# The second head's turn moved ahead of the first head's values, and the last stage moved inside the experts' programs

## The reference, cut to what matters

```python
y = mixer(u)                 # mLSTM heads and 4 latent-attention heads, one output projection
x = post_ln(alpha * x + (1 + g1) * y)            # alpha = 2 ** 0.25
u = layernorm(x) * (1 + sc2) + sh2
y = hier_moe(u)              # top-1 group of 4, then top-2 of its 8 experts
x = post_ln(alpha * x + (1 + g2) * y)            # the output

# latent attention, for a block of 128 queries and one head
s = qn @ kn.T + qr @ kr.T
p = softmax(s * scale)
o = p @ v

# gated experts: every token has two (expert, weight) pairs
out[e] = (silu(x @ w_gate[e]) * (x @ w_up[e])) @ w_down[e]
y[token] = w0 * out[e0][token] + w1 * out[e1][token]
```

## Time and profile before

| | us |
|---|---|
| time, median of 3 runs | 1618.43 (1618.35 to 1618.6) |
| time of the profiled execution | 1616.71 |
| its span | 1614.8 |
| PE busy | 1464.7 (91%) |
| DVE busy | 570.7 (35%) |
| ACT busy | 355.0 (22%) |
| attention loop, first turn to last values | 547 to 747 |
| last block's light down product ends | 1547.6 |
| first transfer of the last stage is issued | 1559.6 |

### The profile page before, as it was taken

One profiled execution on the slowest core, in us unless ns is written; L12 is line 12 of the kernel. 1 busy time (PEld: TensorE's weight loads), 2 busy tenths in 40 slices (PEclk: granted clock), 3 DMA queues, 4 the chain that ended last, 5 costly groups with the idle time before them and its releaser, 6 DMA issues. The chain is left out here.

```text
span 1614.8 us, 19679 instructions
## 1 busy us (share of the span) xinstructions
PE 1464.7 (91%) x7275; PEld 811.3 (50%) x7276; DVE 570.7 (35%) x1134; ACT 355.0 (22%) x735; POOL 97.1 (6%) x96
## 2 busy tenths in 40 slices
PE   5999999979969899998999269999999999999968
PEld 2555554448858456655555244444444444444423
DVE  1122127557749434334776621111111111011117
ACT  2122122146524333433111001011111110110111
POOL 0000011000000000000000011111111111011100
PEclk8999999999979999999999569999999999999979
DMA  9201011228710200003111089969789879999936
GB/s 377 99 27 39 0 7 41 54 75 246 241 56 1 105 0 0 0 0 141 53 66 66 26 343 374 408 236 370 314 345 392 312 317 410 423 358 419 401 149 275
DMA packets 98181, 305.49 MB, mean 189 GB/s; under 512 B 18065, under 2 KB 53053, under 8 KB 88920
## 3 DMA queue, kind: packets, MB, share of 16 engines
q1 hardware_dynamic: 89880, 287.08, 46.0%
q0 software_dynamic: 8064, 16.80, 2.8%
q10 hardware_dynamic: 192, 1.03, 0.2%
HBM read 289.86 MB, written 25.76 MB: 195 GB/s over the span
## 5 line engine op out<-in xcount | busy, mean ns | idle before, releaser
L385 PE MATMUL ps<-w_in_tok,uT 128*128 128x512 f32 (+2 forms) x512 | 191.5, 535 | 1.9 <-ACT uT L317 1.9
L1709 PE MATMUL ps<-w_gate_sb,x_slotsT 128*128 x320 | 144.4, 605 | 9.6 <-issue 9.6
L1725 PE MATMUL ps<-w_down_sb,hidT 128*128 x320 | 148.0, 605 | 0.0
L385 PEld LDWEIGHTS ps<-w_in_tok,uT 128*128 128x128 f32 x512 | 97.7, 192 | 90.2 <-issue 59.6
L1709 PE MATMUL ps<-w_up_sb,x_slotsT 128*128 x320 | 140.6, 592 | 0.0
L1913 DVE TENSOR_TENSOR hid<-silu_g,ps 128x512 f32<-128x512 f32 x20 | 13.8, 688 | 295.4 <-PE ps L1709 295.4
L1420 PE MATMUL ps<-uT,hT 128*128 128x512 f32 x256 | 114.1, 599 | 0.0
L529 PE MATMUL ps<-uT,mod 128*128 128x512 f32 x256 | 111.0, 593 | 0.8 <-PEq L204 0.8
L1709 PEld LDWEIGHTS ps<-w_gate_sb,x_slotsT 128*128 128x128 f32 x320 | 59.9, 192 | 86.9 <-issue 86.9
L1709 PEld LDWEIGHTS ps<-w_up_sb,x_slotsT 128*128 128x128 f32 x320 | 60.8, 190 | 76.5 <-issue 76.5
L1725 PEld LDWEIGHTS ps<-w_down_sb,hidT 128*128 128x128 f32 x320 | 57.5, 189 | 66.5 <-issue 65.6
(11 more groups left out here) (376 smaller groups left out, 1829.6 us busy)
## 6 DMA issues: line engine op xcount, KB each, us to landing
light_gate_sb<-in_w_gate SPq DMA_DIRECT2D x20, 2048.0 KB
light_up_sb<-in_w_up SPq DMA_DIRECT2D x20, 2048.0 KB
light_down_sb<-in_w_down SPq DMA_DIRECT2D x20, 2048.0 KB, 12.9
w_gate_sb<-in_w_gate SPq DMA_DIRECT2D x12, 2048.0 KB, 11.4
w_up_sb<-in_w_up SPq DMA_DIRECT2D x12, 2048.0 KB, 15.6
w_down_sb<-in_w_down SPq DMA_DIRECT2D x12, 2048.0 KB
mod<-in_w_ada SPq DMA_DIRECT2D x8, 1024.0 KB, 8.7
w_ada_late<-in_w_ada SPq DMA_DIRECT2D x8, 1024.0 KB, 7.8
```

The costliest lines, as they stand in the source:

```text
L385: mm = nc.tensor.matmul(ps[:, 2 + g, 0:n], self.uT[:, k, t * P:(t + 1) * P], wt[:, k, c0:c0 + n], start=k == 0, stop=k == KD - 1)
L1709: m = m_.matmul(ps[:, bank, :], xT[:, k, :], wt[:, bass.ds(buf, 1), k, :].rearrange("p a f -> p (a f)"), start=k == 0, stop=k == KD - 1)
L1725: m = m_.matmul(ps[:, 5 + half, :], hT[:, k, :], wd[:, bass.ds(buf, 1), k, half * 512:half * 512 + 512].rearrange("p a f -> p (a f)"), sta ...
```

## The change

In `attend`, PE turns the second head before it computes the values of the first, and DVE copies the second head's half before it scales the first head's output. The waits for the copies move out of `out`. ACT's program stays as it is.

The last stage loses its block. Its code follows the loop in every engine's program of `experts`, its tiles of x go into the gate weights' buffer, its expert rows into the buffers of `wu`, `lwg` and `lwu`, and its results into that of `wd`, each with room for all 8 tiles. The tiles of x are loaded after the last gate product (`s_G`), the expert rows after the last scatter has landed. PE has four pairs of banks for the sums instead of two, and does the residual part (alpha times x) up to three tiles ahead of the expert rows. The two rows of parameters `ln2_g` and `ln2_b` are loaded at the start of the block instead of after SP's loop.

```diff
                 def out(n, h):
                     j = h % 2
-                    pe.wait_ge(s_td, n + 1)
-                    pe.wait_ge(s_ta, n + 1)
                     pe.wait_ge(s_oe, n + 1)
...
                         scores(1 - g)
+                        pe.wait_ge(s_td, n + 1)
+                        pe.wait_ge(s_ta, n + 1)
+                        turn(1)
                         out(n, 2 * g)
-                        turn(1)
+                        pe.wait_ge(s_td, n + 2)
+                        pe.wait_ge(s_ta, n + 2)
                         out(n + 1, 2 * g + 1)
...
                         maximum(0)
                         maximum(1)
+                        turned(n + 1, 1)
                         out(n, t, 2 * g)
-                        turned(n + 1, 1)
                         out(n + 1, t, 2 * g + 1)
...
             @block.sync
+                sp.dma_start(self.g2[:], self.i["ln2_g"].partition_broadcast(P)).then_inc(self.s_again, 16)
+                sp.dma_start(self.b2[:], self.i["ln2_b"].partition_broadcast(P)).then_inc(self.s_again, 16)
...
...
+                sp.wait_ge(s_G, n + 1)
+                for t in range(TT):
+                    sp.dma_start(x1[:, t], self.x1d[t * P:(t + 1) * P, :]).then_inc(s_x1[t], 16)
+                sp.wait_ge(s_yfree, n + 1)
+                sp.wait_ge(s_lyfree, n + 1)
+                for t in range(TT):
+                    sp.dma_start(yt(t), yb[t]).then_inc(s_y[t], 16)
+                for t in range(TT):
+                    sp.wait_ge(s_o, t + 1)
+                    sp.dma_start(self.out[t * P:(t + 1) * P, :], z[:, t]).then_inc(s_st, 16)
...
             @block.tensor
+                def residual(t):
+                    if t > 3:
+                        pe.wait_ge(s_read, t - 3)
+                    pe.wait_ge(s_x1[t], 16)
+                    for half in range(2):
+                        m_.matmul(sums(t, half), al[:], x1[:, t, half * 512:half * 512 + 512], start=True, stop=False)
+                def rows_of_experts(t):
+                    pe.wait_ge(s_y[t], 16)
+                    pe.wait_ge(s_dg, 2 * t + 2)
+                    for k in range(2):
+                        for half in range(2):
+                            m = m_.matmul(sums(t, half), dg[:, t % 2, k, :], yt(t)[:, k, half * 512:half * 512 + 512], start=False, stop=k == 1)
+                    m.then_inc(s_sum, 1)
...
+                residual(0)
+                pe.wait_ge(s_sg, n + 1)
+                pe.wait_ge(s_h, n + 1)
+                residual(1)
+                pe.wait_ge(s_lh, n + 1)
+                pe.wait_ge(s_yd, n + 1)
+                residual(2)
+                pe.wait_ge(s_lyd, n + 1)
+                for t in range(TT):
+                    rows_of_experts(t)
+                    if t + 3 < TT:
+                        residual(t + 3)
```

More of the change, by code:

```diff
@@ L177, in build @@
             self.experts()
-            self.combine()
     def c(self, at, n=P, parts=P):
@@ L1531, in experts @@
         HF = FE // 2
+        s_x1 = [self.sem(f"x1_loaded{t}") for t in range(TT)]
+        s_y = [self.sem(f"pair_loaded{t}") for t in range(TT)]
+        s_cv, s_var, s_std, s_o, s_st = (self.sem(n) for n in ("cb_dve", "varC", "stdC", "out_ready", "out_stored"))
+        s_al, s_dg, s_sum, s_read = self.sem("alpha_diagonal"), self.sem("weight_diagonals"), self.sem("rows_summed"), self.sem("sum_read")
+        yb = self.ybuf.rearrange("(t p k) d -> t p k d", p=P, k=2)
+        SUM_BANKS = (0, 2, 6, 4)
         with ExitStack() as x, nc.Block() as block:
@@ L1573, in experts @@
             col = sb("table_cols", [P, 5])
+            al, dg = sb("alpha_diag", [P, P]), sb("weight_diag", [P, 2, 2, P])
+            st, mv, ve = sb("stC", [P, 2, 6]), sb("mvC", [P, 2]), sb("veC", [P, 2, 2])
+            x1 = wg[:].rearrange("p a k f -> p (a k f)").rearrange("p (t d) -> p t d", t=TT)
+            z = wd[:].rearrange("p a k d -> p (a k) d")
+            pairs = [buf.rearrange("p (t k d) -> p t k d", k=2, d=D) for buf in (
+                wu[:].rearrange("p a k f -> p (a k f)"), lwg[:].rearrange("p k f -> p (k f)"), lwu[:].rearrange("p k f -> p (k f)"))]
+            yt = lambda t: pairs[0][:, t] if t < 4 else pairs[t // 2 - 1][:, t % 2]
+            sums = lambda t, half: ps[:, SUM_BANKS[t % 4] + half, :]
             s_used = (s_G, s_U, s_Y)
@@ L1603, in _ @@
                                          src[bass.ds(e, 1)].rearrange("a p k f -> p (a k) f")).then_inc(s_w[j], 16)
-                sp.dma_start(self.g2[:], self.i["ln2_g"].partition_broadcast(P)).then_inc(self.s_again, 16)
-                sp.dma_start(self.b2[:], self.i["ln2_b"].partition_broadcast(P)).then_inc(self.s_again, 16)
+                sp.wait_ge(s_G, n + 1)
[8 more added lines that the diff above has]
+                    sp.dma_start(self.out[t * P:(t + 1) * P, :], z[:, t]).then_inc(s_st, 16)
+                sp.wait_ge(s_st, 16 * TT)
             @block.gpsimd
@@ L1761, in _ @@
                     m.then_inc(s_lY, 1)
+                def residual(t):
[11 more added lines that the diff above has]
+                    m.then_inc(s_sum, 1)
+                pe.wait_ge(s_al, 1)
+                pe.wait_ge(s_xT, n + 1)
+                pe.wait_ge(s_lxT, n + 1)
+                residual(0)
[10 more added lines that the diff above has]
+                        residual(t + 3)
             @block.scalar
@@ L1765, in _ @@
                 a = nc.scalar
+                ident = self.c(C_ID)
+                a.mul(al[:], ident, ALPHA).then_inc(s_al, 1)
                 act.wait_ge(s_d, 1)
@@ L1787, in _, with diagonals @@
                     a.copy(xlT[:].rearrange("p k t -> p (k t)"), ps[:, 0, 0:KD * LC]).then_inc(s_lxT, 1)
+                def diagonals(t):
+                    if t > 1:
+                        act.wait_ge(s_sum, t - 1)
+                    for k in range(2):
+                        a.mul(dg[:, t % 2, k, :], ident, self.wts[:, k, t:t + 1]).then_inc(s_dg, 1)
+                diagonals(0)
+                for t in range(TT):
+                    if t + 1 < TT:
+                        diagonals(t + 1)
+                    act.wait_ge(s_var, t + 1)
+                    a.activation(ve[:, t % 2, 1:2], ve[:, t % 2, 0:1], ACT.Sqrt).then_inc(s_std, 1)
             @block.vector
@@ L1926, in _ @@
                     v.tensor_tensor(yl[:], ps[:, 4, 256:256 + Q], gate2q[:], ALU.mult).then_inc(s_lyd, 1)
[L1927 to L2007, removed]
@@ L2008, in _ @@
+                cb = Chain(dve, s_cv)
                 dve.wait_ge(self.s_again, 32)
                 for t in range(TT):
-                    b, j = t % B, t % 2
-                    rows = ps[:, 2 * j:2 * j + 2, :].rearrange("p a b -> p (a b)")
+                    j, bank = t % 2, SUM_BANKS[t % 4]
+                    rows = ps[:, bank:bank + 2, :].rearrange("p a b -> p (a b)")
                     dve.wait_ge(s_sum, t + 1)
-                    ch.link(v.bn_stats(st[:, 0, :], ps[:, 2 * j, :]))
@@ L2014, in _ @@
-                    ch.link(v.bn_stats(st[:, 1, :], ps[:, 2 * j + 1, :]))
-                    ch.link(v.bn_aggr(mv[:], st[:].rearrange("p a b -> p (a b)")))
+                    cb.link(v.bn_stats(st[:, 0, :], sums(t, 0)))
+                    cb.link(v.bn_stats(st[:, 1, :], sums(t, 1)))
+                    cb.link(v.bn_aggr(mv[:], st[:].rearrange("p a b -> p (a b)")))
                     v.tensor_scalar_add(ve[:, j, 0:1], mv[:, 1:2], LN_EPS).then_inc(s_var, 1)
-                    if t >= B:
-                        dve.wait_ge(s_st[b], 16 * (t // B))
@@ L2019, in _ @@
-                    v.scalar_tensor_tensor(out=z[:, b], in0=rows, scalar=mv[:, 0:1], in1=g2[:], op0=ALU.subtract, op1=ALU.mult).then_inc(s_read, 1)
+                    v.scalar_tensor_tensor(out=z[:, t], in0=rows, scalar=mv[:, 0:1], in1=self.g2[:], op0=ALU.subtract, op1=ALU.mult).then_inc(s_read, 1)
                     dve.wait_ge(s_read, t + 1)
                     dve.wait_ge(s_std, t + 1)
-                    ch.link(v.reciprocal(ve[:, j, 1:2], ve[:, j, 1:2]))
-                    v.scalar_tensor_tensor(out=z[:, b], in0=z[:, b], scalar=ve[:, j, 1:2], in1=b2[:], op0=ALU.mult, op1=ALU.add).then_inc(s_o, 1)
+                    cb.link(v.reciprocal(ve[:, j, 1:2], ve[:, j, 1:2]))
@@ L2027 @@
+                    v.scalar_tensor_tensor(out=z[:, t], in0=z[:, t], scalar=ve[:, j, 1:2], in1=self.b2[:], op0=ALU.mult, op1=ALU.add).then_inc(s_o, 1)
 SHAPES = {
```

## The result

The changed kernel takes 1598.49 us (median of 4 runs, 1595.71 to 1601.71) against 1618.51 before, a ratio of 0.9876 with an interval of 0.9855 to 0.9896, so 20.0 us less. The profiled execution took 1597.24 us, its span is 1595.4 (before: 1616.71 and 1614.8).

| stretch, us | before | after |
|---|---|---|
| start to the first turn of attention | 546.97 | 545.70 |
| attention, first turn to the end of the last values | 199.74 | 189.79 |
| from there to the first matmul of the router's ranking | 167.59 | 168.21 |
| from there to the end of the last light down product | 633.31 | 633.10 |
| from there to the end of the span | 67.19 | 58.60 |

What follows compares the result with a forecast made beforehand. PE, busy nine tenths of the span, was taken as the bound, with its waits in attention and before the last stage. Attention 9.5 plus last stage 11.0 gave 20.5 us, so 1597.9 us; forecast 1595 to 1602, range 1594 to 1606.

Steps and rivals of the forecast that it cites:

- the loop step: Attention, step over the loop's end: its excess of 0.74 us goes, 7 steps, 5.2 us; 3.4 if only the wait goes.
- DVE's order: Attention: the second head's copy starts right behind both maxima, gaining 0.27 us for each of 16 groups, 4.3 us.
- (b): Last stage: residuals of three tiles, 5.2 us, fit before the rows land; PE leaves its loops in 3 to 4 us.
- (c): Last stage, low clock after PE's gap: about 1 us in the sum, with 0 and 2.7 as bounds.
- (a): Last stage, expert rows: first load issued at about 1552.0, takes 4.6 to 5.6 us, rows there at 1556.6 to 1557.6.
- (d): Last stage, final tiles: DVE sets the end, 39.5 us from the first sum on instead of 40.7, gaining 1.2 us.
- PE arrives late: Rival, last stage: PE leaves its loops only at 1559.6; time 1607.3, half as late 1602 to 1603; chance 0.15.
- the 1.5 us for seven rounds: Last stage: by the skill's branch times, seven empty loop rounds cost PE about 1.5 us, not 3 to 4.
- The loop step keeps its excess: Rival, attention: the 0.74 us is loop control, not ACT; 5.2 us less gain, 1603.1 us; chance 0.12.
- PE becomes the bound of attention: Rival, attention: needs the copy ahead of the maxima; 10.1 us more gain, 1587.8 us; chance 0.03.
- Reads of PSUM collide: Rival, attention: ACT's probabilities and DVE's maximum slow each other; 1628.3 us with maximum and copy doubled; chance 0.03.

Runs made afterwards that it cites:

- Experiment 1: Only the attention edits (PE's and DVE's order) made in the kernel before, last stage as it was: 1606.47 us against 1617.36, ratio 0.9941.
- experiment 3: Changed kernel with DVE's old order in attention (scaling of the first head ahead of the second head's copy) and PE's new one: 1606.78 us, ratio 0.9941.
- experiment 9: The changed kernel run again unchanged, for its spread: 1597.6 us, ratio 0.9881.
- Experiment 4: Changed kernel with residual matmuls only one tile ahead of the expert rows instead of three: 1596.22 us, ratio 0.9875.
- experiment 8: Kernel before with POOL's unrolled program cut from 48 to 24 block rounds: 1613.1 us in its one run.
- experiment 7: Changed kernel with GROUP = 16 for 8, so 12 empty inner and 1 empty outer round instead of 4 and 3: 1602.6 us in one run.
- experiment 5: Changed kernel with DVE copying the second head between the two maxima instead of behind both: 1584.01 us against 1617.94, ratio 0.979.
- experiment 6: Changed kernel with DVE's copy between the maxima and residual matmuls only one tile ahead, together: 1582.69 us, ratio 0.9789.
- experiment 10: Changed kernel with copy between the maxima, residuals one tile ahead and GROUP = 24, so 1 empty outer round instead of 3: 1583.22 us, ratio 0.9791.
- experiment 2: The whole change with the old order in attention, so the last stage's change alone: 1609.57 us, ratio 0.9947.

## Why the prediction was right, and where it wasn't

Predicted were 1597.9 us, measured 1598.49; against the profiled executions the sum was 20.5 and the difference is 19.5. The near hit in the total hides one term that was too large, and in part it is luck: the last stage was put 2.4 us too high, attention 0.45 too low, and 0.9 came from stretches that the sum leaves at nothing.

**Attention, 9.5 predicted, 9.95 measured.** The waits came out as said: 0.62 us 16 times, and hardly one for ACT but the first. A round takes 23.42 us (594.79 to 618.21; said: 23.5). Experiment 1 shows that all of it comes from these hunks. Taking the whole 0.74 of the loop step, not only the named 0.49, was right: both steps are 11.71 now. What the prediction had not seen is that PE's order needs DVE's. It priced DVE's order at 0.27 us a group; given PE's order it is worth 0.5 (4.03 less 3.50), 8.5 us in all, for experiment 3 shows the scaling waiting for values that the early turn had put off. PE's order alone, priced at 5.2 for the loop step, gave 1.4.

**Last stage, 11.0 predicted, 8.6 measured (10.1 in the second profile of the same kernel).** The failed step is (b) with (c), "residuals start at about 1551 and end at 1556 at full clock", and 1 us for the clock. PE's idle was 4.47, not 3 to 4, and the low clock cost 8.19 - 5.15 = 3.0 us (1.6 in experiment 9), above the 2.7 that the prediction gave as a bound; that bound itself reads 2.6 from start to start. So the residuals, not the rows' landing, decided when the first sum was complete: 16.3 us after PE's last product where 13.7 was said and 23.5 was before. That is a gain of 7.2 us instead of 9.8, inside the bounds of 7.1 to 11.1, and of 8.7 in experiment 9. In (a) the shortest load took 4.8 us, as said, but the first was issued 3.3 us after that product and not 4.4, so the rows were there 1 us sooner than said, which was worth nothing. The step on DVE's last tiles (d) said 1.2 us, and it is 43.59 - 42.22 = 1.4 from the start of DVE's first tile to the end of the span.

Step (d) also held the clue that the prediction passed over. Behind the loops PE has a fixed 96 passes; doing three residuals first only shifts which work comes last, and leaves DVE three tiles that it can't follow. The gain in the end is better counted so: PE starts 15.61 - 4.47 = 11.1 us sooner, loses 0.5 to a costlier low clock, and 2.1 to DVE's back-to-back tiles, 8.5 in all. Experiment 4 takes the lead away and gets the 2.1 back, with 0.8 from the clock.

**The rivals.** *PE arrives late*: not true in its strong form, PE was out in 4.5 us. In the kernel before POOL was the last, which experiment 8 shows for 0.77 us only. The mechanism, though, is real: experiment 7 puts a price of 0.72 us on a round. So the 1.5 us for seven rounds that the prediction works out from the times of single branches is too low; seven come to about 5.1 us (an estimate from the traces), close to the 5.8 of SP's queue. The Trainium skill's rule on fetched branch targets (Runtime: NRT & Kernel Launch, Instruction fetch mechanics) isn't needed for it: the idle follows the count of rounds, 2.96, 4.47 and 8.80 us for 5, 7 and 13. *The loop step keeps its excess*: not true. *PE becomes the bound of attention*: not by this change, but experiment 5 makes it so, with the copy ahead of one maximum and not of both as the prediction asked. It was worth 13.5 us instead of the 10.1 priced. *Reads of PSUM collide*: not true, 1.22 us for the maximum beside ACT's probabilities.

The prediction took 3.2 us as about what tells a change from none. Single runs of the changed kernel lie up to 6.0 us apart (1595.71 to 1601.71), its two medians 0.9 (1598.49 and 1597.6), so this holds for medians and not for single runs.

## What to carry to other kernels

When a wait shrinks by less than its length, look at what stands ahead of the releasing instruction on its own engine. Here, moving the copy one line further up (experiment 5, 13.5 us) was worth more than both edits of attention together (9.95). Two engines' orders belong together: moving work on one can make the other's old order wait, as in experiment 3. Work done ahead of a late arrival fills the wait, but it also changes what is left for last. Here PE's last two tiles had no residual part, DVE could not follow them, and the end was 2.1 us longer for it.

## What the runs showed that was not expected

An empty round of a loop with a test costs PE 0.72 to 0.75 us: (8.80 - 4.47) / 6 between experiment 7 and the change, (4.46 - 2.96) / 2 between experiments 6 and 10. The second pair differs by outer rounds alone, the first by 8 inner ones more and 2 outer ones less, which makes an inner round 0.73. Seven such rounds are 5.1 us, 0.6 more than the idle of 4.47, so some of them passed beside the last product (an estimate). Before the last stage was moved, the block's end hid these rounds.

The length of the idle said little about what the low clock costs behind it. Read from start to start as above, it cost 1.6 to 3.1 us after an idle of 4.4 to 4.5 us (five traces: the result 3.0, experiments 2, 3, 5 and 9 with 3.1, 1.7, 3.1 and 1.6), 2.9 after 8.80 us in experiment 7, and 2.6, 2.7 and 3.1 after 15.6, 15.5 and 14.7 us in the kernel before and experiments 1 and 8.

Kernels that are the same up to attention reach its first turn between 544.32 and 548.19 us in twelve traces. That 4 us is of the size of the spread of single runs. Attention itself took 189.75 to 189.81 us in the five traces with its new order. So the stretches of the traces, not the medians, separate effects of 2 us here.
